# Weight-block products cut into two halves, with expert products between them

## The reference

```
for l in range(DEPTH):                      # DEPTH = 2
    h = rmsnorm(x, norm_mix_g[l])
    z = h @ w_in[l]                         # queries, keys, values, gates, conv and pool inputs
    x = x + concat(nsa(z), conv(z), pool(z)) @ w_out[l]
    q = rmsnorm(x) @ xa_wq[l];  k, v = split(rmsnorm(mem) @ xa_wkv[l])      # 256 memory tokens
    x = x + cross_attention(q, k, v) @ xa_wo[l]
    h = rmsnorm(x)
    q = h @ peer_wq[l]                      # 8 heads; scores against 2 x 128 sub-keys
    # 16 of 128 x 128 experts for each head and token:
    act = gelu(dot(h, u[expert]))           # u, v: rows of 1024 numbers
    x = x + sum(gate * act * v[expert])
return rmsnorm(x, final_g)
```

## Time and profile before

| what | value |
|---|---|
| median of three runs | 1790.23 us |
| the profiled execution | 1803.4 us, of which the span is 1801.6 |
| TensorE busy (products) | 1334.3 us, 74% of the span |
| VectorE busy | 1111.0 us, 62% |
| ScalarE busy | 490.4 us, 27% |
| GpSimd busy | 663.8 us, 37% |
| moved by DMA | 701.66 MB, mean 389 GB/s |
| mean granted TensorE clock | 0.864 of full speed |

### The profile page before, as it was taken

One profiled execution on the slowest core, in us unless ns is written; L12 is line 12 of the kernel. 1 busy time (PEld: TensorE's weight loads), 2 busy tenths in 40 slices (PEclk: granted clock), 3 DMA queues, 4 the chain that ended last, 5 costly groups with the idle time before them and its releaser, 6 DMA issues. The chain is left out here.

```text
span 1801.6 us, 22636 instructions
## 1 busy us (share of the span) xinstructions
PE 1334.3 (74%) x8260; PEld 681.1 (38%) x8260; DVE 1111.0 (62%) x2763; ACT 490.4 (27%) x1290; POOL 663.8 (37%) x1028
## 2 busy tenths in 40 slices
PE   7999876669999847667778757667878656565554
PEld 5856742235564523222364433223454421111110
DVE  5510588895343757798444767798434758954444
ACT  3411132253212222225222222226322212211111
POOL 0000224344333433345333434444424344465551
PEclk9999988689999979878989979888989876787777
DMA  9742699999999999999999999999999989999996
GB/s 391 291 174 87 275 395 423 392 397 417 424 423 422 422 396 422 422 413 421 424 421 422 420 416 423 420 405 421 422 423 422 421 360 421 403 407 421 421 421 258
DMA packets 87519, 701.66 MB, mean 389 GB/s; under 512 B 10097, under 2 KB 10225, under 8 KB 12145
## 3 DMA queue, kind: packets, MB, share of 16 engines
q0 software_dynamic: 73728, 536.90, 72.0%
q1 hardware_dynamic: 13680, 163.32, 22.0%
HBM read 698.09 MB, written 2.10 MB: 389 GB/s over the span
## 5 line engine op out<-in xcount | busy, mean ns | idle before, releaser
L499 POOL DMA_INDIRECT uv_rows<-uv_in,idx x512 | 504.3, 985 | 1087.7 <-PE acc_pe L1265 844.6
L1265 PE MATMUL acc_pe<-uv_rows,diag 64*64 64x512 f32 x4096 | 614.9, 729 | 346.5 <-ACT diag L999 331.5
L540 DVE CUSTOM_DVE_ANT_0 uv_rows<-uv_rows,h_ps 128x1024 f32<-128x1024 f32 x512 | 609.1, 1218 | 267.9 <-DMA uv_rows<-uv_in,idx 262.1
L1265 PEld LDWEIGHTS acc_pe<-uv_rows,diag 64*64 64x64 f32 x4096 | 154.0, 153 | 719.8 <-ACT diag L999 505.0
L993 ACT ACTIVATE gelu_b<-act_b 128x2 f32<-128x2 f32 x256 | 52.2, 204 | 783.6 <-DVE act_b L540 771.2
L1292 PE MATMUL bank<-w_ring,h_t 128*128 128x512 f32 x400 | 189.0, 628 | 17.9 <-DMA w_ring<-blocks_in 12.3
L1292 PEld LDWEIGHTS bank<-h_t,w_ring 128*128 128x128 f32 x1600 | 182.1, 193 | 20.7 <-issue 18.1
L1292 PE MATMUL bank<-h_t,w_ring 128*128 128x128 f32 x1600 | 186.4, 278 | 2.2 <-DMA w_ring<-blocks_in 1.2
L493 POOL TENSOR_TENSOR diag<-ident_st,gate 128x64 f32<-128x64 f32 x512 | 159.3, 312 | 14.7 <-DVE gate L933 5.2
L999 ACT ACTIVATE diag<-diag,gelu_b 128x64 f32<-128x64 f32 x512 | 151.2, 342 | 8.6 <-ACT gelu_b L993 0.2
L1292 PEld LDWEIGHTS bank<-w_ring,h_t 128*128 128x128 f32 x400 | 78.4, 201 | 129.2 <-issue 104.7
(11 more groups left out here) (204 smaller groups left out, 1137.2 us busy)
## 6 DMA issues: line engine op xcount, KB each, us to landing
w_ring<-blocks_in SPq DMA_DIRECT2D x62, 2048.0 KB
uv_rows<-blocks_in SPq DMA_DIRECT2D x9, 2048.0 KB, 15.1
uv_rows<-uv_in,idx POOLq DMA_INDIRECT x512
tcon<-tile_consts_in SPq DMA_DIRECT2D x4, 656.5 KB, 10.5
uv_rows<-blocks_in SPq DMA_DIRECT2D x2, 1024.0 KB, 8.5
h_ffn<-ffn_gain_in SPq DMA_DIRECT2D x4, 512.0 KB, 28.5
xs<-x_in SPq DMA_DIRECT2D x2, 512.0 KB, 17.2
uv_rows<-mem_in SPq DMA_DIRECT2D x1, 1024.0 KB, 14.8
```

Source lines behind the costliest of these rows:

```text
L499: nc.gpsimd.indirect_dma_start(uv_rows[:, slot_of(k), :, :].rearrange("p a n -> p (a n)"), None, a["uv"], bass.IndirectOffsetOnAxis(ap=idx ...
L540: v.tensor_tensor_reduce(u_row, u_row, h_ps[:, :], 1.0, 0.0, ALU.mult, ALU.add, act_b[:, k // B % AHEAD, k % B:k % B + 1]).then_inc(sems[" ...
L1265: mm = pe.matmul(acc_pe[c * HT:(c + 1) * HT, r * BLK:(r + 1) * BLK], diag[tok, slot_of(k), :], uv_rows[tok, slot_of(k), 1, c * BLK:(c + 1) ...
```

## The change

Outside of stage A each product with a weight block becomes two steps. `half_X` opens the job and does the first half of the matmuls, `X` does the second half and closes the job. A product that adds up over eight chunks of the depth is cut after the fourth; one that writes four column groups is cut after the second. The weights in `LENGTH` are cut with it: 4 becomes 2 + 2, 8 becomes 4 + 4, and `wo` and `xo` go from 9 to 4 + 4, so that the sum of the weights falls from 321 to 317 in `PLAN` and from 385 to 381 in `MEM_PLAN`. `spread` then deals out the 62 batches anew, for all engines.

```diff
+HALVES = ["ab", "zq", "zk1", "zk2"] + [f"{name}{i}" for name, n in (("wo", 2), ("xq", 2), ("xo", 2), ("pq", 4),
+                                                                      ("mem_kv", 8)) for i in range(n)]
+HALF_JOBS = {**{f"half_{name}": STEP_JOBS[name] for name in HALVES}, **{name: [] for name in HALVES}}
...
-        "win_values0", "win_values1", "win_out", "small_branches", "mix_turn", "wo0", "wo1", "xa_norm", "xq0", "xq1",
...
+        "win_values0", "win_values1", "win_out", "small_branches", "mix_turn", "half_wo0", "wo0", "half_wo1", "wo1",
+        "xa_norm", "half_xq0", "xq0", "half_xq1", "xq1", "xa_scores", "xa_turn", "xa_out", "half_xo0", "xo0",
...
-LENGTH = {"mix_norm": 4, "ab": 4, "zq": 4, "zk1": 4, "zk2": 4, "conv_in": 0, "conv": 2, "rope": 3, "branch_gates": 0,
+LENGTH = {"mix_norm": 4, "ab": 2, "zq": 2, "zk1": 2, "zk2": 2, "conv_in": 0, "conv": 2, "rope": 3, "branch_gates": 0,
...
-          "win_out": 2, "small_branches": 3, "mix_turn": 2, "wo": 9, "xa_norm": 7, "xq": 8, "xa_scores": 6,
-          "xa_turn": 4, "xa_out": 4, "xo": 9, "ffn_norm": 8, "pq": 8, "sub_scores": 2, "mem_kv": 8}
+          "win_out": 2, "small_branches": 3, "mix_turn": 2, "wo": 4, "xa_norm": 7, "xq": 4, "xa_scores": 6,
+          "xa_turn": 4, "xa_out": 4, "xo": 4, "ffn_norm": 8, "pq": 4, "sub_scores": 2, "mem_kv": 4}
...
-                    def rows_product(job, w, lhs):
-
-                        close_job(product(open_job(job)[:, :], [(lhs[:, c, :], w[:, c, :]) for c in range(KC)]), job)
+                    def rows_product(job, name, lhs, part):
+
+                        if part == 0:
+                            need_weights(name)
+                            open_job(job)
+                        out, w = bank_of(job), weights(name)
+                        for c in range(part * KC // 2, (part + 1) * KC // 2):
+                            mm = pe.matmul(out[:, :], lhs[:, c, :], w[:, c, :], start=(c == 0), stop=(c == KC - 1))
+                        if part == 1:
+                            close_job(mm, job)
+
+                    def cols_half(job, name, part):
+
+                        if part == 0:
+                            need_weights(name)
+                            open_job(job)
+                        out, w = bank_of(job), weights(name)
+                        for o in range(2 * part, 2 * part + 2):
+                            mm = product(out[:, o * P:(o + 1) * P],
+                                         [(w[:, c, o * P:(o + 1) * P], h_t[:, c, :]) for c in range(KC)])
+                        if part == 1:
+                            close_job(mm, job)
...
+                    for name in HALVES:
+                        if first:
+                            steps[name] = lambda name=name: both(parts[name])
+                        else:
+                            steps["half_" + name] = lambda name=name: parts[name](0)
+                            steps[name] = lambda name=name: parts[name](1)
```

More of the change, by code:

```diff
@@ new lines @@
+PLAN = ["mix_norm", "half_zq", "zq", "rank1", "rank_more1", "half_ab", "ab", "rank_pairs1", "rank_pairs_more1",
[3 rows of a table added]
+        "cmp_hidden", "cmp_hidden_turn", "conv0", "conv1", "cmp_kv", "conv2", "conv3", "cmp_scores", "sel_scores",
+        "sel_more", "sel_exps", "cmp_probs", "conv4", "conv5", "cmp_out", "sel_turn", "win_scores", "win_more",
+        "win_exps", "conv6", "conv7", "sel_values0", "sel_values1", "sel_out", "conv_norm", "win_turn", "conv_act",
[5 rows of a table added]
+MEM_PLAN = ["mix_norm", "half_zq", "zq", "rank1", "rank_more1", "half_ab", "ab", "rank_pairs1", "rank_pairs_more1",
+            "look_up1", "look_up_more1", "conv_in", "gates1", "half_zk1", "zk1", "rank2", "rank_more2",
+            "rank_pairs2", "rank_pairs_more2", "look_up2", "look_up_more2", "half_zk2", "zk2", "rope", "rank3",
+            "rank_more3", "turn_kv", "rank_pairs3", "rank_pairs_more3", "branch_gates", "gates2", "gates3",
+            "look_up3", "look_up_more3", "cmp_in", "cmp_hidden", "cmp_hidden_turn", "conv0", "conv1", "cmp_kv",
+            "conv2", "conv3", "cmp_scores", "sel_scores", "sel_more", "sel_exps", "cmp_probs", "conv4", "conv5",
+            "cmp_out", "sel_turn", "win_scores", "win_more", "win_exps", "conv6", "conv7", "sel_values0",
+            "sel_values1", "sel_out", "conv_norm", "win_turn", "conv_act", "win_values0", "win_values1", "win_out",
+            "small_branches", "mix_turn", "half_wo0", "wo0", "half_wo1", "wo1", "xa_norm", "half_xq0", "xq0",
+            "half_xq1", "xq1", "xa_scores", "xa_turn", "xa_out", "half_xo0", "xo0", "half_xo1", "xo1",
+            "half_mem_kv0", "mem_kv0", "half_mem_kv1", "mem_kv1", "half_mem_kv2", "mem_kv2", "half_mem_kv3",
+            "mem_kv3", "half_mem_kv4", "mem_kv4", "half_mem_kv5", "mem_kv5", "half_mem_kv6", "mem_kv6",
+            "half_mem_kv7", "mem_kv7", "ffn_norm", "half_pq0", "pq0", "sub_scores0", "rank0", "rank_more0",
+            "half_pq1", "pq1", "rank_pairs0", "rank_pairs_more0", "sub_scores1", "look_up0", "look_up_more0",
+            "gates0", "half_pq2", "pq2", "sub_scores2", "half_pq3", "pq3", "sub_scores3"]
@@ L1523, in mix_turn, with wo @@
                         turn("OT", [o_sum[:, c * P:(c + 1) * P] for c in range(4)])
[L1525 removed]
+                    def wo(i, part):
                         pe.wait_ge(sems["cat_ready"], 1)
[L1527 removed]
+                        rows_product(f"WO{i}", f"wo{i}", cat_t, part)
                     def xa_scores():
@@ L1558, in xa_out, with xo, both @@
                             close_job(mm, f"XO{i}")
-                    def xo(i):
+                    def xo(i, part):
                         pe.wait_ge(sems["xo_ready"], 2)
-                        rows_product(f"XW{i}", need_weights(f"xo{i}"), xo_t)
+                        rows_product(f"XW{i}", f"xo{i}", xo_t, part)
+                    def both(parts):
+                        parts(0)
+                        parts(1)
                     def sub_scores(job, lo, n, copies):
```

76 lines of the change are left out of this document (33 added, 43 removed), and 13 rows, old and new, of the table PLAN.

## The result

The changed kernel takes 1801.64 us (median of nine runs, 1799.71 to 1805.11), the kernel before 1792.95 in nine runs (1786.97 to 1799.05). The ratio is 1.0047, 95% interval 1.0031 to 1.0062: slower by 8.4 us, where 4 us less were predicted. The profiled execution of the changed kernel is 1801.45 us, its span 1799.7.

The account below looks back on a forecast made before the run. The prediction took full DMA engines (422 GB/s) as the bound: 1803.4 + 0 (cuts) - 3 (end of stage B) - 1 (new deal) = 1799.4 us; the -4 carried to the median 1790.2 gave 1786, range 1776 to 1799.

Parts of the forecast that it names:

- the batches dealt out anew: Stages B, C and D: batches moved to other steps change DMA idle time; taken at -1 us, between -5.6 and +8.6.
- the crowding at `cmp_in`: Stages C and D: with the batch before cmp_in gone, TensorE frees no buffer for longer; at most +8.6 us.
- the sign of a hole of more than 3 us at `cmp_hidden`: Stages C or D: a DMA hole above 3 us there was listed as showing the forecast wrong.
- These windows are bytes over rate, so nothing there can cost.: 405 to 585, 855 to 1035, 1260 to 1440 us: DMA full at 421 or 422 GB/s, TensorE's order changes nothing; 0.
- some 20 us: Ten buffers in flight hold 25 us of DMA work, so TensorE can hold them back some 20 us.
- The end of stage B, -3: Cutting pq2 and pq3 frees buffers 3.7 us earlier and closes the DMA hole there; -3 us, between 0 and -3.1.
- The cut products, 0: wo to pq, stages B, C and D: all but the last lie where DMA has no idle time; 0 us.
- The end of D "stays": The 6.6 us DMA hole at stage D's end remains, since the halves of pq2 and pq3 stand side by side there.
- Rival 1: Stages B, C and D: all holes go except stage D's end, 14.6 us saved, time 1776; chance 0.18.
- Rival 2: Stage B: weight blocks come late and TensorE becomes the bound, +15 us, time 1801; chance 0.08.
- Rival 3: Stage B: the 14 cut products restart at a lower clock, 31 us lost, time 1817; chance 0.03.
- Rival 4: Nothing that can be told: stage B's hole shifts into C, crowding and extra batch cancel, time 1790; chance 0.25.

Follow-up runs that it names:

- d_e: Kernel before, products uncut, stage D only: a batch put between the two halves of sel_values and between those of win_values; ratio 1.0004.
- d_f: Kernel before, uncut, stage D only: batches behind sel_out and conv_norm, none between win_turn and conv_act, one more ahead of wo0, value halves together; ratio 1.0002.
- d_i: Kernel before, uncut, stage D only: value halves parted as in d_e, no batch between win_turn and conv_act, no extra batch ahead of wo0; ratio 1.0037.
- d_a: Kernel before, uncut, with the new deal of batches only in stage D's steps up to conv3; ratio 0.9986.
- cut: Kernel before with the change's cut products, but batches dealt as before (wo and xo weigh 4 and 5); ratio 0.9978.
- cut_b: Kernel before with products cut in stage B only, batches dealt as before; ratio 0.9993.
- cut_x: As cut, plus batches moved in stages C and D behind xq1, xo1 and pq1; ratio to the kernel before 0.9981.
- deal: Kernel before with the change's new deal of batches in stages B, C and D, no product cut; ratio 1.0055.
- mend: The changed kernel with the batches from sel_values0 to mix_turn dealt as before in stages B, C and D; ratio to the kernel before 0.9993.

## Why the prediction was wrong

**The step that failed: "the batches dealt out anew", taken at -1 us with bounds of -5.6 and +8.6.** Measured alone it is +0.55%, 9.9 us (6.8 to 12.9): the wrong sign, and a middle outside of the bound. The step counted batches in stretches ("one batch more done at the same step up to `wo0`") and priced two things, VectorE's extra 2.4 us and the crowding at `cmp_in`. It never read which two steps each moved batch now separates. The list of the deal shows that a batch fell between the halves of `sel_values` and `win_values`, that VectorE's next operation needs both, and that a batch on TensorE, 1.95 us at least, now lies in its way; and that the batch between `win_turn` and `conv_act` went. That was readable before the run; that the two cost something only together (d_e 1.0004, d_f 1.0002, d_i 1.0037) was not. The crowding, which got the upper bound, costs nothing (d_a); the sign of a hole of more than 3 us at `cmp_hidden` did come in D (3.9), without the cost. TensorE does wait longer for `cmp_in` in stage C, as the earlier trace rows would let one fear, and the window 765 to 855 moves 421 for all that:

```profile
771.21 5.29 DVE L715 TENSOR_TENSOR area<-kv_t,smalls 64x128 f32<-64x128 f32 x16
...
776.55 5.81 PE L1435 MATMUL bank<-w_ring,area 128*32 128x256 f32 x64 [3.88 <-DVE area L715]
```

**"These windows are bytes over rate, so nothing there can cost."** Failed as a rule, in D: 409 where 422 were. A saturated window was read as an immune one. Its reserve is the landed and unfinished rows of ten buffers, the "some 20 us" of the prediction; how much of it a stretch of stops uses up was not measured. Stage C has the same deal, and its window 855 to 1035 still moves 422. A likely reason, not tried apart, is that its value halves are x8 instead of x16: TensorE takes 1.10 us for each of the two halves of `win_values`, and VectorE waits at line 787 once, 3.8 us at `sel_out`, against 11.0 in two stops in D:

```profile
856.25 1.10 PE L1300 MATMUL bank<-kv_n,area 128*128 128x64 f32 x8
...
860.25 1.10 PE L1300 MATMUL bank<-kv_n,area 128*128 128x64 f32 x8
```

**The end of stage B, -3.** The mechanism is there. Windows and waits, answering to the earlier trace rows:

```profile
639.00:642.00 3.00, 3.00 (x29) 1.28 (x31) 1.73 (x3) 1.48 (x4) 1.15 (x2) 1.00 0.98 410
642.00:645.00 3.00, 2.83 (x28) 0.67 (x20) 0.32 (x3) 0.79 (x3) 2.65 (x5) 1.00 1.01 399
```

```profile
633.79 0.97 POOL L507 DMA_INDIRECT uv_rows<-uv_in,idx  x1 [9.94 <-PE acc_pe L1273]
...
640.82 0.97 POOL L507 DMA_INDIRECT uv_rows<-uv_in,idx  x1 [4.29 <-PE acc_pe L1273]
```

No window is under 350 GB/s, as asked. The sign "no wait over 7 us" failed: it is 9.94. But GpSimd gets two rows out from 633.79 on and then waits 4.29, which is enough. The gain in DMA work, some 3 us (419 to 421 instead of 392 to 404 in 65 us), is there in `cut`, `cut_b` and `cut_x`, and not in `deal`. The sign "stage B shorter by 3 to 5 us" failed: it takes 431.7 us, against 427.4 and 424.5 in the two profiles of before. In `cut` it takes 420.5. The forecast of 3 us fits the 4 us of `cut`, without being proven for this place.

**The cut products, 0.** Nothing speaks against it: `cut` is 0.22% faster as a whole, and its windows 405 to 585, 855 to 1035 and 1260 to 1440 move 422 or 423. VectorE's waits at line 820 fell by 16.4 us, less than the 20 to 40 expected, and those for landing rows fell by 13.2 where they should have risen, while those at line 787 rose by 16.3. In `cut`, without the new deal, the signs are those of the prediction: 135.7 us for `wo` and `xo` (20.3 less), 267.3 for landing rows (5.2 more).

**The end of D "stays".** 418 GB/s now against the earlier trace rows's 329, and 401 in the second profile of before. How deep that hole is varies from one execution to the next (6.6 and 1.5 us in one and the same kernel), and the base of 1803.4 was high, in part by it; carrying the difference to the median was right, and the median of before has since stood at 1792 to 1798.

**Rivals.** Rival 1 (holes go, 1776): no. Rival 2 gave 1801, and the time is 1801.6, for another reason: between 405 and 600 us TensorE waits for no block at all. Rival 3 (clock, in stage B): no, 0.99 in 405 to 585 and also in `cut`. The Trainium skill's advice ("TensorE: Matmul & The Clock Gate", HAM oscillation) is to do a product's depth tiles in one go, before waiting for a DMA; here going against it does no harm as long as matmuls of a batch fill the cut. The clock does fall in stage D, but not at a cut product: none stands before 1290, and `deal`, which cuts nothing, is granted 0.66 to 0.89 between 1245 and 1290 as the change is. Rival 4 (nothing) is what `mend` does. `wo0` in C, answering to the earlier trace rows: 5.40 us for its first half after a wait of 2.14, at first below the full clock as before.

## What to carry to other kernels

When a rule deals work between steps, read for every moved batch the pair of steps it now parts, and ask whether another engine's next instruction needs both; adjacent halves of one result want to stay together. A window in which the DMA engines are full is not safe ground: moves that cost nothing alone (1.0004, 1.0002) cost 0.4% together. Test moves in pairs before calling any of them free, and when a change alters both an instruction order and a table of weights, time each alone: here the one gained 0.2% and the other lost 0.5%.

## What the runs showed of the hardware that I had not expected

A batch (x16 of 64x512) takes 1.95 us at 2.4 GHz and 3.69 us at the lower level of 1.2 GHz (granted clock 0.50), and the x16 of 128x64 take 2.00 and 3.67. Waits of TensorE of 2 to 2.4 us often stand before such slow pieces, but not always (2.08, then 1.95, at 1282.31 in the second profile of before), and what follows differs: behind a wait of 2.39 us d_i is at the lower level from 1272.8 to 1280.1, and d_f for one batch. The pieces of a loss in stage D measured +0.04, +0.02 and -0.17% and together +0.31%. And two profiled executions of one kernel differ by 10.5 us of span (1801.6 and 1791.1), 6.9 us of it in stage D, with 5.1 less missing DMA work at its end. Stage A, whose order is the same in all twenty profiles here, takes from 219.1 to 229.5 us.
